# The last norm, the token rows and the routing of a mixture of experts, made in one block

## The reference, cut to what matters

```python
x = x + gate_m * (merged @ w_out[l])
h = rms_norm_2(x, norm_ffn[l]) * (1.0 + scale_f) + shift_f
# hier_moe(h): 4 groups of 8 experts
group_logits = hf @ w_group + b_group
g_sel = argmax(group_logits); p_group = softmax(group_logits)[g_sel]
exp_logits = (hf @ w_router + b_router).reshape(n, 4, 8)
top_p, top_i = top_k(softmax(exp_logits[g_sel]), 2)
weights = p_group * top_p / sum(top_p)
# every token goes to 2 experts; the 2048 pairs are sorted by expert and
# padded to blocks of 128 slots: slot_tok[48 * 128], block_expert[48]
xb = h_pad[slot_tok].reshape(48, 128, 1024)
yb = (silu(xb @ w_gate[e]) * (xb @ w_up[e])) @ w_down[e]   # per block
y = segment_sum(yb * slot_w, slot_tok)
```

## Time and profile before

| what | us |
|---|---|
| median of three runs (4586.13 to 4586.83) | 4586.62 |
| span of the profiled execution | 4584.7 |
| last DVE instruction of the mixer's projection ends | 3671.44 |
| first instruction of the stages that change | 3672.14 |
| first logits matmul | 3749.60 |
| last DVE instruction of the routing, about | 3813.4 |
| first transpose of gathered rows in `experts` | 3851.18 |

### The profile page before, as it was taken

One profiled execution on the slowest core, in us unless ns is written; L12 is line 12 of the kernel. 1 busy time (PEld: TensorE's weight loads), 2 busy tenths in 40 slices (PEclk: granted clock), 3 DMA queues, 4 the chain that ended last, 5 costly groups with the idle time before them and its releaser, 6 DMA issues. The chain is left out here.

```text
span 4584.7 us, 42478 instructions
## 1 busy us (share of the span) xinstructions
PE 3953.7 (86%) x16276; PEld 2819.4 (61%) x16276; DVE 2099.5 (46%) x2655; ACT 1550.5 (34%) x2451; POOL 673.8 (15%) x332
## 2 busy tenths in 40 slices
PE   4799799999798799996857899889999855999996
PEld 1687455568586355583636666567777744666664
DVE  0391466651372566622356423233442213666665
ACT  1412345550422445413141335222220012555542
POOL 0221200002221100020101010123333222011111
PEclk9899899999899799987988899999999966999997
DMA  4211100111210121222312110233333234999975
GB/s 165 74 37 30 35 19 29 32 42 65 78 47 26 42 66 56 65 83 53 40 40 52 45 21 10 42 75 83 88 86 68 74 112 129 359 352 358 353 290 213
DMA packets 346632, 451.05 MB, mean 98 GB/s; under 512 B 51965, under 2 KB 221106, under 8 KB 344898
## 3 DMA queue, kind: packets, MB, share of 16 engines
q1 hardware_dynamic: 331186, 405.28, 29.3%
q0 software_dynamic: 12656, 25.26, 1.5%
q10 hardware_dynamic: 2592, 17.83, 1.0%
HBM read 408.39 MB, written 59.31 MB: 102 GB/s over the span
## 5 line engine op out<-in xcount | busy, mean ns | idle before, releaser
L1144 PE MATMUL values<-probs,vp 128*128 128x512 f32 x672 | 348.6, 600 | 12.0 <-issue 6.4
L1232 ACT ACTIVATE probs<-scores 128x512 f32<-128x512 f32 (+1 forms) x336 | 196.0, 583 | 306.3 <-PE scores L219 304.6
L217 PE MATMUL scores<-q_hi,k_rest 97*128 97x512 f32 (+1 forms) x336 | 262.3, 781 | 0.0
L3382 PE MATMUL dp<-h_t,abt 128*128 128x512 f32 x544 | 241.9, 598 | 1.1 <-ACT abt L3431 0.9
L261 POOL TENSOR_TENSOR ring_r<-ring_w,ring_hi 128x1024 fp32r<-128x1024 f32 x44 | 136.8, 3111 | 702.5 <-ACT ring_hi L254 702.5
L3413 ACT ACTIVATE expert_hi<-wu 128x1024 fp32r<-128x1024 f32 x136 | 144.8, 1065 | 251.4 <-PE gp L219 251.4
L1313 DVE TENSOR_REDUCE mx<-made 128x1 f32<-128x640 f32 (+1 forms) x272 | 203.9, 794 | 27.2 <-PE made L1085 26.4
L217 PE MATMUL smb<-x_t_r,merge_w_r 128*128 128x512 f32 x480 | 196.1, 408 | 22.2 <-POOL merge_w_r L2723 19.4
L217 PE MATMUL gates_ps<-x_t_r,ring_r 128*128 128x512 f32 (+1 forms) x560 | 206.5, 369 | 2.5 <-PEq L83 2.5
L734 DVE SCALAR_TENSOR_TENSOR conv_out<-conv_in,vectors,conv_out 128x1295 f32<-128x1295 f32 (+1 forms) x120 | 205.9, 1716 | 4.3
L218 PE MATMUL gates_ps<-h_t_r,ring_hi 128*128 128x512 f32 (+1 forms) x560 | 206.4, 369 | 0.0
(11 more groups left out here) (527 smaller groups left out, 9504.9 us busy)
## 6 DMA issues: line engine op xcount, KB each, us to landing
wg<-in_w_gate SPq DMA_DIRECT2D x34, 2048.0 KB, 9.8
wu<-in_w_up SPq DMA_DIRECT2D x34, 2048.0 KB, 11.0
h_t<-in_w_down SPq DMA_DIRECT2D x34, 2048.0 KB, 9.9
ahead_w<-in_w_ada SPq DMA_DIRECT2D x48, 512.0 KB, 3.9
ring_w<-in_w_in SPq DMA_DIRECT2D x44, 512.0 KB, 4.0
mod_w<-in_w_mod ACTq DMA_DIRECT2D x8, 1536.0 KB, 29.1
ahead_w<-in_w_mod SPq DMA_DIRECT2D x24, 512.0 KB, 3.5
out_w<-in_w_out SPq DMA_DIRECT2D x24, 512.0 KB, 5.2
```

Source lines behind the costliest of these rows:

```text
L217: nc.tensor.matmul(out, lhs[1], rhs[0], start=start, stop=False, **kw)
L1144: nc.tensor.matmul(O[b % 2][:, 0:w], vp[g // 2 % 2][:, kb, g % 2 * VD:g % 2 * VD + P], pr[m % 3][:, 0:w], start=kb == 0, stop=kb == nk - 1 ...
L1232: nc.scalar.activation(pr[m % 3][:, 0:w], S[m % 2][:, 0:w], ACT.Exp, scale=scale).then_inc(s.exped, 1)
L3382: m = nc.tensor.matmul(dp[half][:, :], at[:, j, :], wd[u][:, j, half * 512:(half + 1) * 512], start=j == 0, stop=j == FK - 1)
```

## The change

The stages 1 to 5 become one stage, `ffn_route`, with one barrier at its end, and parts of stage 6 move into it.

- The rows are made token-major from the start: PE transposes `x` itself (not `h`), ACT squares a tile of 128 tokens straight from PSUM with an accumulated sum for each token, takes ln and exp on 128x1, and DVE multiplies the transposed tile by the root (one number for each partition) and by the factor, spread over the partitions once. POOL adds the shift row, SP stores. The tiles lie in the memory of `k.h`.
- The logits come from raw `x`: the factor is multiplied into the router's weights (`fw`), 36 stationary columns and 512 moving ones in 16 matmuls, between the transposes of the tiles. The shift's part is a constant for each column (`const_ps`), the root multiplies afterwards.
- Ranks and counts are matmuls of rounded 0/1 data, `both` against `before_r` and `ones_r`, 16 of them in place of 44.
- The slot table is a product of 0/1 matrices: DVE writes for each of the 16 columns of pairs where in its block the pair lies (`lane`, 128 wide) and which block it is, times its token value (`blocks_r`, 2 x 48 wide); 16 rounded matmuls add them up in PSUM, and one DVE instruction puts the table into `slot_tokens`. The DRAM table, its fill, the sixteen indirect DMAs and the read back are gone.
- The loads of routing constants stand ahead of the expert prefetch on SP, the down weights of experts 0 and 1 behind the stores of the rows, and POOL clears `xb` at the start of the stage.

The core of the difference:

```diff
@@ new function ffn_route: SP, POOL, PE
+            for u in range(2):
+                for dst, src, sem in ((r.wg[u], a.w_gate_2, r.gate_in[u]), (r.wu[u], a.w_up_2, r.up_in[u])):
+                    sp.dma_start(dst[:, :, :], src[0, u].rearrange("(k p) n -> p k n", p=P)).then_inc(sem, 16)
+            for t in range(T):
+                sp.wait_ge(s.shifted, t + 1)
+                sp.dma_start(r.rows[t * P:(t + 1) * P, :], rows[:, t, :]).then_inc(s.stored, 16)
+            sp.wait_ge(s.stored, 16 * T)
+            for u in range(2):
+                sp.dma_start(r.wd[u], a.w_down_2[0, u].rearrange("(k p) n -> p k n", p=P)).then_inc(r.down_in[u], 16)
...
+            for t in range(T):
+                if t == 0:
+                    pool.wait_ge(s.kept1, 1)
+                pool.wait_ge(s.rowed, t + 1)
+                nc.gpsimd.tensor_tensor(rows[:, t, :], rows[:, t, :], s_rows[:, :], ALU.add).then_inc(s.shifted, 1)
...
+            def turn_tile(t):
+                if t >= 2:
+                    pe.wait_ge(s.rowed, t - 1)
+                for j in range(DK):
+                    m = nc.tensor.transpose(x_ps[t % 2][:, j * P:(j + 1) * P], k.x[:, j, CTX + t * P:CTX + (t + 1) * P],
+                                            k.ident)
+                m.then_inc(s.turned, 1)
...
+            pe.wait_ge(s.kept1, 1)
+            pe.wait_ge(s.weighted, 1)
+            for j in range(DK):
+                raw_logits(j)
+                if j + 2 < T:
+                    turn_tile(j + 2)
@@ ranks: PE
-                for i in range(t + 1):
-                    m = nc.tensor.matmul(rank_ps[:, t, :], k.mats[:, BEFORE, :] if i == 0 else k.ones[:, :],
-                                         both[:, t - i, :], start=i == 0, stop=i == t)
+            nc.tensor.matmul(rank_ps[:, :, :], before_r[:, :], both[:, :, :], start=True, stop=False)
+            for d in range(1, T):
+                nc.tensor.matmul(rank_ps[:, d:T, :], ones_r[:, :], both[:, 0:T - d, :], start=False, stop=d == T - 1)
...
+            for n in range(CH):
+                if n % T == 0:
+                    pe.wait_ge(s.places_ready, 2 if n else 1)
+                m = nc.tensor.matmul(table_ps[:, :, :], lane[:, n, :], blocks_r[:, n, :, :], start=n == 0, stop=n == CH - 1)
@@ ACT
+            for t in range(T):
+                act.wait_ge(s.turned, t + 1)
+                nc.scalar.activation(lane_f[:, 0:DK, :].rearrange("p a b -> p (a b)"), x_ps[t % 2], ACT.Square,
+                                     accum_out=ss[:, t:t + 1]).then_inc(s.squared, 1)
+                act.wait_ge(s.squared, t + 1)
+                step(nc.scalar.activation(ss[:, t:t + 1], ss[:, t:t + 1], ACT.Ln, bias=k.eps, scale=1.0 / D))
+                nc.scalar.activation(rt[:, t:t + 1], ss[:, t:t + 1], ACT.Exp, scale=-0.5).then_inc(s.rooted, 1)
@@ DVE
+                V.scalar_tensor_tensor(rows[:, t, :], x_ps[t % 2], rt[:, t:t + 1], f_rows[:, :], ALU.mult, ALU.mult)\
+                    .then_inc(s.rowed, 1)
...
+                step(V.tensor_tensor(lane[:, at, :], row(IOTA_LANE, P, True, T),
+                                     place[:, 0, at].unsqueeze(2).broadcast_to([P, T, P]), ALU.is_equal))
+                step(V.tensor_tensor(spot, row(IOTA_BLOCK, NB, True, T),
+                                     place[:, 1, at].unsqueeze(2).broadcast_to([P, T, NB]), ALU.is_equal))
...
+            dve.wait_ge(s.table_made, 1)
+            V.tensor_scalar(r.idx[:, 0:NB, :], table_ps.rearrange("p c b -> p b c"), float(2 * SEQ), None, ALU.add)\
+                .then_inc(r.table_in, 1)
@@ POOL
-            for i in range(2):
-                for t in range(T):
-                    pool.indirect_dma_start(r.table, bass.IndirectOffsetOnAxis(ap=r.slot[:, i, t:t + 1].bitcast(U32), axis=0),
-                                            tok[:, t, 2 * i:2 * i + 2], None).then_inc(s.scattered, 16)
-            pool.wait_ge(s.scattered, 16 * (2 * T + 1))
```

More of the change, by code:

```diff
@@ L3074, in _, with raw_logits @@
         @block.tensor
         def _(pe):
-            pe.wait_ge(s.loaded, 80)
+            def turn_tile(t):
[5 more added lines that the diff above has]
+                m.then_inc(s.turned, 1)
+            def raw_logits(j):
+                for b in range(2):
+                    m = nc.tensor.matmul(raw_ps[:, b, :], fw[:, j, :], k.x[:, j, CTX + 512 * b:CTX + 512 * (b + 1)],
+                                         start=j == 0, stop=j == DK - 1)
+                m.then_inc(s.raw_made, 1)
@@ L3092, in _ @@
+            m.then_inc(s.table_made, 1)
         @block.scalar
@@ L3257, in _ @@
             def _(sp):
-                with nc.allow_non_contiguous_dma("a column of indices to each block"):
-                    sp.dma_start(idx[:, 0:N_BLOCKS, :], r.table.rearrange("(b p) o -> p b o", p=P)).then_inc(s.table_in, 16)
                 def load(dst, src, e, sem):
```

228 lines of the change are left out of this document (123 added, 105 removed).

## The result

The changed kernel takes 4466.77 us (median of four runs, 4465.14 to 4470.45) against 4586.61 before (4586.13 to 4586.83). The ratio is 0.9738, with a 95% interval of 0.9724 to 0.9752: 2.6% faster. The forecast was 4471 in a range of 4463 to 4485. A second measurement of the unaltered kernel gave 4462.9 and a ratio of 0.9732 (0.9698 to 0.9765).

What follows compares the result with a forecast made beforehand. The prediction took the chain of stages ahead of the experts as the bound. Its steps brought the first gathered rows from 3851.2 to 3735.9, 115.3 us less: span 4469.4, with 1.9 around it 4471; range 4463 to 4485.

Steps and rivals of the forecast that it cites:

- The last rival: Experts run slower through other addresses and DMA share 1.01, making the whole slower than before, 4596 us; chance 0.02.
- First load to first raw logits: Start of the block: constants land 4.9 us after first issue, DVE multiplies the router's weights in 0.46; 5.5 us.
- The tile loop: Raw logits and tile transposes, 3677.6 to 3700.4: PE sets the pace at 2.9 us a tile.
- The rival of the low clock: PE's clock stays at its lower level through the tile loop: 20 us more, 4491; chance 0.12 for most of it.
- Choice, ranks, slots, table: Routing steps behind the logits, up to the written slot table: 8.4, 3.6, 5.0 and 9.1 us.
- Behind the table: From the table instruction to the first gather's issue: six tiny instructions 1.3 us, barrier 0.7.
- Gather: First gather's issue to its rows at PE: 4.5 us, bounds 3.2 to 7.8, with down weights already loaded.
- DVE behind POOL: Rival: DVE's choice, with two SBUF operands, stops behind a late POOL addition: +3 us, 4474; chance 0.08.
- constant: The shift's constant behind the tile loop, 8 matmuls of 36 columns, 16 records: 1.7 us, bound 3.4.
- tiny activations: ACT's two tiny activations for tile 0's root, estimated at 0.25 us each; bounds -1 and +1.
- transposes: PE's transposes taken at 1.15 us each tile; 0.9 instead would give -2.
- hand-overs: Passing work between engines at some twenty places, 0.05 to 0.2 us each; bound +2.

Runs made afterwards that it cites:

- the second trace: The changed kernel measured and traced once more, with no edit: 4462.9 us, ratio 0.9732.
- the dummy work: Changed kernel plus PE transposing the unit matrix 60 times during the choice, 60 behind the ranks, 50 ahead of the first `xb`: 4472.09 us, ratio 0.9746.
- The late down weights: Changed kernel, but SP issues the down weights of experts 0 and 1 only once the slot table is made: 4471.74 us.
- The doubled additions: Changed kernel, but POOL does a second addition of two SBUF tiles, same size, behind each of its eight: 4476.13 us.
- the split loads: Changed kernel, but router's weight loads have their own semaphore; biases and index constants are waited for only behind the rows: 4467.96 us, ratio 0.9730.
- the kernel with 44 matmuls: Changed kernel with ranks and counts made as before, by 44 unrounded fp32 matmuls (88 records): 4477.11 us.

## Why the prediction was right

**The frame held.** A microsecond taken from the chain was a microsecond of the total: the experts, 733.5 us before, take 732.35. The last rival, slower experts, is out, and in no kernel did the tail grow beyond 735.9.

**First load to first raw logits, 5.5 forecast, 7.71 measured: the step that was off most.** The forecast took the landing of the constants from the earlier trace rows, where no large transfer was in flight. There the index constants (38 KB) landed 2.7 us after their own issue; here (102 KB) it was 4.9, with 8 MB of prefetch issued right behind them. Which of the two is the reason wasn't tried. In the eleven other kernels and traces with the same load in the same company it was 3.1 to 4.1, so the 4.9 is the slowest of twelve, and part of this miss is chance. The edit that waits only for the weights brought the start to 4.0.

**The tile loop, 22.8 forecast, 22.2 measured, out of two errors that cancel.** The first chunk took 3.30 instead of 1.78, because PE had been idle and the clock fell; the wait of 1.6 for the first row didn't come, because PE began late enough. That the sum came out is luck: in the second trace, where neither the fall nor the wait came, the loop took 20.9. Then PE paces the loop with 2.86 us a tile (2.9 forecast: 1.91 and 1.09, overlapping slightly). ACT's extra record for reading the accumulated sum, 0.19 to 0.21 us, had no term; it is hidden under PE. The rival of the low clock was right in kind and wrong in extent: one chunk, not eight. What the forecast held against it, gaps of PE under 2 us ahead of the loop, did not hold: the gap was 3.98.

**Choice, ranks, slots, table: 8.4, 3.6, 5.0, 9.1 forecast; 8.43, 3.80, 5.14, 8.96 measured.** These terms came from counts of instructions and the duration of the same instruction before. Undone one by one, the table gives back 20.5 us and the ranks 15.4.

**Behind the table, 2.0 forecast, 3.21 measured.** The barrier was taken as the 0.7 us between DVE's end and the next stage's first load. But here the first gather comes 2.15 us behind DVE's end: 1.3 to PE's first instruction and 0.9 more until POOL's gather, as the dummy work shows. At the border ahead of the block PE and POOL started 0.7 us behind DVE's end, so it isn't the barrier alone; what fills the rest isn't shown.

**Gather, 4.5 forecast, 4.49 measured**, chosen between 3.2 and 7.8. The late down weights gave 7.7.

**DVE behind POOL, chance 0.08.** It didn't happen: an addition took 2.35 us and not 3.1, POOL's last one ends at 3696.19, and the pass over `logits` that would be held starts at 3697.41. The cover is 1.2 us. The rival bounded the price by the time that POOL still works when the choice begins, and one instruction more. The doubled additions bear that out: POOL worked on for 13.95 us behind DVE's first instruction on the logits, and the choice came 13.3 later.

**The size.** The stretch is 66.5 us against 63.8, the tail 1.2 less: with the start at 3672.14 the span would be 4471.0 and the time 4472.9. The profiled execution took 4465.14, because its block began 7.7 us earlier. The forecast had no term for that, though the starts spread over 16.5 us, nearly the width of its range: with this block and tail, the earliest start (3656.0) would have given some 4457, below the range, and the latest (3672.5) 4473. That the total lies within is owed to the terms of the block and, in part, to luck with the start. What moves the start stays open. In all fourteen traces the last matmul of the first transformer block's output projection starts between 2069.4 and 2074.6, and the second one's first (L218) between 3563.0 and 3579.3, so the differences arise in the second block, ahead of its output projection. Repeated runs of one kernel differ by some 10 us too (4459.66 to 4469.86 for the split loads), so both the build and the execution may have a part in it, and whether some of the 7.7 us is the edit's own doing isn't settled.

**The range.** The parts that the forecast lists add up to -4.3 and +8.0 us (gather -1.3 and +3.3, constant +1.7, tiny activations -1 and +1, transposes -2, hand-overs +2), not to the -7 and +9 that it writes. By its own parts the lower end would have been 4467.0, and the measured 4466.77 would have lain just below it. What took it so low is the start, which isn't among the parts.

## What to carry to other kernels

Where small stages form a chain, add up the chain, not the engines' work: count the records of each small matmul at the clock that the chain leaves PE, and look whether a barrier waits for an engine that only issues DMA. Let what starts early wait only for the loads that it needs, and keep large transfers out of the way of a small urgent one: 4 MB issued 3 us ahead of the gather cost 3.3 us. Judge an edit by the stretch that it touches when the rest of the program moves by more than the edit.

## What the runs showed of the hardware that was not expected

A DVE instruction with two SBUF operands was held for 13.79 us by six POOL additions of 2.39 us that followed each other: it got no turn between them. In the kernel before, a POOL instruction lasted 14.26 us in place of 2.33 beside a row of DVE instructions without a gap. With two gathers issued by POOL ahead of a barrier, PE went on only 5.4 us after the second issue had ended and 1.2 us after that gather had landed, while a barrier with 4 MB of SP's loads in flight opened as usual. PE's clock read 0.50 through 18.9 us of unbroken work in the kernel with 44 matmuls. And stages that no edit touched ended anywhere from 3656 to 3672.5 us.
